# Inverse with needed columns only and its first products between the turns; four output tiles ended one by one, their next weights split first

## The chip, the cores and the metric

One Trainium2 chip; the program runs on 1 core. The metric is the device time of one execution in microseconds (us), lower is better.

## What is computed

Two small transformer stacks one after the other on 256 tokens (272 with 16 meta tokens), width 1024, all in float32: forgetting attention and a convolved FFN, a gated DeltaNet layer and another FFN, then an MLA layer and a MoBA layer.

```python
def first_block(x, meta_tokens, ...):
    h = jnp.concatenate([meta, x], axis=1)
    for i in range(DEPTH):                      # DEPTH = 2
        a = rmsnorm(h, norm_mix_pre[i])
        m = forgetting_attention(a, ...) if i % 2 == 0 else gated_deltanet(a, ...)
        h = h + rmsnorm(m, norm_mix_post[i])
        f = conv_ffn(rmsnorm(h, norm_ffn_pre[i]), ffn_w_up[i], ffn_conv[i], ffn_w_down[i])
        h = h + rmsnorm(f, norm_ffn_post[i])
    return h[:, N_META:]

def second_block(x, ...):
    for layer in range(DEPTH):
        y = mla_mixer(x, ...) if layer < N_A else moba_mixer(x, ...)   # each ends in ... @ w_o
        x = layer_norm(ALPHA * x + y, ln_g[layer], ln_b[layer])
    return x
```

The change touches two things in it: the products with the output weights of the four mixers (`@ w_out`, `@ w_o`), and, in the gated DeltaNet, the inverse of a unit triangular matrix that each chunk of each head needs.

## The kernel before

**Weights.** All weights stream through four buffers of 1024 columns (`raw`). For products in three passes each buffer is split: ScalarE copies it to `w_hi` in the rounded format (L359, `split_hi`), VectorE subtracts (`w_lo`, L364, `split_lo`), and TensorE makes hi*hi, hi*lo and lo*hi products (L378 to L380, `product`). A buffer may be split again only when its products are done (semaphore `chunk_used`); SyncE loads the next one when the lower half is done (`lo_done`).

**Output products.** An output weight has two units of four buffers; buffer `j % 4` makes output tile `j` of 8, over 8 blocks `k` of the input (24 products). Tiles 0 to 3 stand in four banks of PSUM. Tile 4 needs buffer 0 again, so it waits until tile 0 is done, then for the split. In `tail_pe` (attention, MLA, MoBA) tiles 0 to 2 are made up to `k = 6` between the steps of the last heads, then tile 3 up to `k = 6`, and then `k = 7` of all four. In the DeltaNet (`w_dn_out`) `k` is the outer loop, tiles 0 to 3 the inner one. In `out_act` (attention and DeltaNet) ScalarE copies a tile out (`m`, L677), squares it for the norm (`sq`, L680) and then splits the buffer; in `ln_act` (MLA, MoBA) it only splits, and VectorE copies out (L715).

**The inverse.** For each of 8 heads (`DNH`) there are 3 chunks of 96 rows. `d_in` holds the inverse so far, `d_tr` its transpose, `a_tr` the matrix. Blocks of 8 on the diagonal come first: `compact` gathers them (L1497), ScalarE copies them (`low`, L1784), seven products (L1519) feed a chain of 14 short VectorE instructions on `q_raw`/`k_raw`, and L1955 expands the result to `d_in`, one instruction a head. Then four levels double the block (8, 16, 32, 64). In a level, step `n` is one head: `x_of(n)` multiplies `a_tr` and `d_in` into `x` (L1534), VectorE masks it into `x_st` (L1967), `update(n)` multiplies `x_st` and `d_tr` (L1548), VectorE subtracts it from `d_tr` (L1979), and `turn(n)` transposes (L1557) so that ScalarE can renew `d_in` (L1791). All three stand in one loop of TensorE, shifted by two and three steps. Before level 1 all eight `turn`s of the expanded blocks run, since `x_of` waits for `d_in`'s semaphore. Levels 3 and 4 work on parts of the array (`part_of`: L1531, L1545, with VectorE's L1965 and L1977). Now and then a transpose of the values (`turn_values`, L1472) stands between.

`keep_clock(30, 3)` puts 30 products that nobody reads (L500) between the seven products and the turns. After the inverse the recurrence runs over the chunks (`c = 0, 1, 2`): three products a head for `c = 0` (L1602, L1610, L1614), five for `c = 1` (with L1588, L1609), four for `c = 2`; then the output product of the layer.

Of the kernel before, what the change touches and what calls it, by code (L numbers as in the profile page):

```python
# [9 lines left out]
ALU = mybir.AluOpType  # L10
# [35 lines left out]
def tables():  # L46
# [30 lines left out]
    def causal(blocks):  # L77
        parts = []
        for q0, q1 in blocks:
# [10 lines left out]
           for b in (BASE << n for n in range(LEVELS - 3))]  # L90
# [86 lines left out]
def build(nc, x, table, params, w, out):  # L177
# [7 lines left out]
    with ctx:  # L185
# [380 lines left out]
        def tail_pe(pe, f, wname, norm, cols, mean):  # L566
# [22 lines left out]
            part(3, 0, last)  # L589
            for j in range(4):  # L590
                part(j, last, KT)
            add(0)
# [75 lines left out]
        def out_act(act, wname, norm, cols):  # L668
# [3 lines left out]
            def tile(j, r):  # L672
                dst = bank[4 + r if "down" in wname else j % 4]
                if KIND[wname] == "down":
                    split(j)
                act.wait_ge(chunk_used, out_tile_done(wname, j))
# [4 lines left out]
                if KIND[wname] != "down":  # L681
                    split(j)
# [716 lines left out]
        def dn_pe(pe):  # L1399
# [112 lines left out]

# [8 lines left out]
            keep_clock(30, 3)  # L1521

            def x_of(n):
                pe.wait_ge(dn["d_in"], n - DNH + 1)
                wait(pe, dn["x_out"], n - DNH - 1)
                part = part_of(n)
                for c in range(NC):
                    cc = slice(c * C, (c + 1) * C)
                    if part:
                        lo, hi = part  # L1530
                        mm = nc.tensor.matmul(sub(bank[n % 2][hi], c, lo), sub(a_tr[lo, n % DNH, :], c, hi),  # L1531
                                              sub(d_in[lo, n % DNH, :], c, lo), start=True, stop=True)
                    else:
                        mm = nc.tensor.matmul(bank[n % 2][0:C, cc], a_tr[:, n % DNH, cc], d_in[:, n % DNH, cc], start=True, stop=True)  # L1534
                mm.then_inc(dn["x"], 1)

            def update(n):
                pe.wait_ge(dn["x_out"], n - DNH + 1)
                pe.wait_ge(dn["d"], n - 1)
                part = part_of(n)  # L1540
                for c in range(NC):
                    cc = slice(c * C, (c + 1) * C)
                    if part:
                        lo, hi = part
                        mm = nc.tensor.matmul(sub(bank[2 + n % 2][lo], c, hi), sub(x_slot(n)[hi], c, lo),  # L1545
                                              sub(d_tr[hi, n % DNH, :], c, hi), start=True, stop=True)
                    else:
                        mm = nc.tensor.matmul(bank[2 + n % 2][0:C, cc], x_slot(n)[:, cc], d_tr[:, n % DNH, cc], start=True, stop=True)  # L1548
# [10 lines left out]
            for n in range(LEVELS * DNH + 4):  # L1559
                if DNH <= n < LEVELS * DNH:  # L1560
                    x_of(n)
                if DNH <= n - 2 < LEVELS * DNH:
                    update(n - 2)
                back = n - (0 if n < DNH else 3)
                if n < DNH or DNH <= back < (LEVELS - 1) * DNH:
                    turn(back)
# [69 lines left out]
            for k in range(KT):  # L1636
                pe.wait_ge(dn["olo"], k + 1)
                for j in range(4):
                    out_part(pe, "w_dn_out", "post2", o_op, TAIL, None, False, j, [k])

# [183 lines left out]
        def dn_dve(dve, st):  # L1824
# [126 lines left out]
            for n in range(DNH):  # L1951
# [3 lines left out]
                nc.vector.tensor_tensor(full, own, blocks_of, ALU.mult).then_inc(dn["d"], 1)  # L1955
            for n in range(DNH, LEVELS * DNH + 2):
                if n < LEVELS * DNH:
                    lv = n // DNH
                    dve.wait_ge(dn["clear"], min(lv, LEVELS - 3))
                    wait(dve, dn["dd"], n - DNH - 1)  # L1960
                    dve.wait_ge(dn["x"], n - DNH + 1)
                    masks = tb("levels")[:, (lv - 1) * C:lv * C].unsqueeze(1).to_broadcast([C, NC, C]) if lv < LEVELS - 2 else None
                    if part_of(n):
                        lo, hi = part_of(n)
                        nc.vector.tensor_copy(sub_all(x_slot(n)[hi], lo), sub_all(bank[n % 2][hi, 0:TP], lo)).then_inc(dn["x_out"], 1)  # L1965
                    else:
                        nc.vector.tensor_tensor(lower(by_chunk(x_slot(n)), lv), lower(by_chunk(bank[n % 2][0:C, 0:TP]), lv),  # L1967
# [446 lines left out]
```

## Time and profile before

| | us |
|---|---|
| Median of 3 runs | 1238.79 (1238.43 to 1240.93) |
| The profiled execution, its own time | 1245.05 |
| Its span, first to last instruction | 1243.3 |
| TensorE busy in it | 1183.2 (95%) |
| VectorE busy | 854.2 (69%) |
| ScalarE busy | 707.2 (57%) |

Times in the trace are us from the start of the span. A row of the timeline is one instruction or several alike in a row: start, duration, engine and line, output and inputs, count; the brackets name how long the engine stood idle before it and who ended that. The profiler shows a float32 product as two records of TensorE (a transpose as one), so that three chunks give `x6`. "PEclk" is the granted TensorE clock: 1.00 is 2.4 GHz, 0.50 is 1.2 GHz.

### The profile page before, as it was taken

To read this page: it belongs to the slowest core of one execution; us is meant where nothing else is said; L and a number is where in the kernel's file an instruction comes from. 1 tells how busy PE (TensorE), PEld (TensorE's weight loads), DVE (VectorE), ACT (ScalarE), POOL (GpSimd) and SP (SyncE) were. 2 spreads that over 40 slices of the span, in tenths; PEclk is the share of its full clock that TensorE was granted. 3 is DMA by queue.
4 is the path that set the end of the run, shared out by engine and by line. 5 is a ranking of instruction groups with operands and counts; after the bars stand their busy time and mean duration, and the time that the engine had idled before them with its cause. 6 is when DMAs were issued, how large, how long until landed. Compare 5 with 4: busy or idle time off the path is not lost.

```text
span 1243.3 us, 27522 instructions
## 1 busy us (share of the span) xinstructions
PE 1183.2 (95%) x10101; PEld 1112.5 (89%) x10101; DVE 854.2 (69%) x1673; ACT 707.2 (57%) x1465; POOL 58.2 (5%) x64
## 2 busy tenths in 40 slices
PE   5999998999999999998998899999999999999996
PEld 4888887999999889988897799999988998899995
DVE  4888875777764487876434677875457876778874
ACT  6776755566654468664334566665545665555543
POOL 0000000122100000001000011110000000000000
PEclk9999998999999999998969899999999999999998
DMA  7333324355555444530100446556635443444431
GB/s 249 128 118 119 101 85 136 97 173 169 173 167 165 118 148 155 173 120 2 35 1 2 136 136 186 184 162 187 194 98 154 123 135 119 136 153 135 135 119 35
DMA packets 50087, 160.35 MB, mean 129 GB/s; under 512 B 5504, under 2 KB 8448, under 8 KB 49888
## 3 DMA queue, kind: packets, MB, share of 16 engines
q1 hardware_dynamic: 50016, 159.37, 41.3%
q8 instruction: 48, 0.79, 0.3%
q14 instruction: 23, 0.19, 0.0%
HBM read 158.30 MB, written 1.05 MB: 128 GB/s over the span
## 4 chain that ended last, share of the span: by engine, by line
PE 88%; DVE 5%; ACT 4%; issue 1%; DMA 1%; SPq 0%; POOL 0%; ACTq 0%; DVEq 0%
PE banks L378 24%; PE banks L380 22%; PE banks L379 22%; PE banks L500 2%; PE banks L917 2%; ACT w_hi L359 2%; PE banks L453 1%; PE banks L897 1%; DVE w_lo L364 1%; PE banks L882 1%; DVE m L533 1%; PE banks L1557 1%; PE banks L879 1%; PE banks L1602 1%; PE banks L1485 1%
## 5 line engine op out<-in xcount | busy, mean ns | idle before, releaser
L364 DVE TENSOR_TENSOR w_lo<-raw,w_hi 128x1024 fp32r<-128x1024 f32 (+5 forms) x332 | 370.2, 1121 | 194.1 <-ACT w_hi L359 193.0
L378 PE MATMUL banks<-x_hi,w_hi 128*128 128x272 f32 (+2 forms) x1624 | 477.7, 294 | 7.1 <-DVE x_lo L513 3.4
L379 PE MATMUL banks<-x_lo,w_hi 128*128 128x272 f32 (+2 forms) x1624 | 464.6, 286 | 0.0
L380 PE MATMUL banks<-x_hi,w_lo 128*128 128x272 f32 (+2 forms) x1624 | 464.4, 286 | 0.0
L359 ACT ACTIVATE w_hi<-raw 128x1024 fp32r<-128x1024 f32 (+5 forms) x332 | 314.5, 955 | 93.0 <-PE banks L380 87.1
L378 PEld LDWEIGHTS banks<-x_hi,w_hi 128*128 128x128 f32 x1624 | 307.4, 189 | 19.1 <-issue 9.1
L379 PEld LDWEIGHTS banks<-x_lo,w_hi 128*128 128x128 f32 x1624 | 308.4, 190 | 0.1
L380 PEld LDWEIGHTS banks<-x_hi,w_lo 128*128 128x128 f32 x1624 | 307.7, 189 | 0.0
L378 PE MATMUL banks<-hid_hi,w_hi 128*128 128x272 f32 (+1 forms) x352 | 101.3, 288 | 0.0
L380 PE MATMUL banks<-hid_hi,w_lo 128*128 128x272 f32 (+1 forms) x352 | 99.8, 284 | 0.0
L379 PE MATMUL banks<-hid_lo,w_hi 128*128 128x272 f32 (+1 forms) x352 | 99.8, 284 | 0.0
L1022 ACT ACTIVATE p_e<-s_m,mx 128x128 f32<-128x128 f32 (+3 forms) x112 | 48.0, 429 | 70.2 <-DVE mx L1126 70.2
L378 PE MATMUL banks<-o_hi,w_hi 128*128 128x256 f32 (+2 forms) x256 | 77.3, 302 | 6.7 <-DVE w_lo L364 5.5
L1381 POOL TENSOR_TENSOR hid<-g_e,u_y 128x272 f32<-128x272 f32 (+1 forms) x44 | 48.8, 1110 | 574.9 <-ACT g_e L1325 574.9
L380 PE MATMUL banks<-o_hi,w_lo 128*128 128x256 f32 (+2 forms) x256 | 73.8, 288 | 0.0
L379 PE MATMUL banks<-o_lo,w_hi 128*128 128x256 f32 (+2 forms) x256 | 73.7, 288 | 0.0
L1350 DVE SCALAR_TENSOR_TENSOR g_y<-banks,par,g_y 128x271 f32<-128x271 f32 (+1 forms) x88 | 43.3, 492 | 44.2 <-ACT u_y L1318 38.5
L378 PEld LDWEIGHTS banks<-hid_hi,w_hi 128*128 128x128 f32 x352 | 66.1, 188 | 1.1
L379 PEld LDWEIGHTS banks<-hid_lo,w_hi 128*128 128x128 f32 x352 | 66.4, 189 | 0.0
L380 PEld LDWEIGHTS banks<-hid_hi,w_lo 128*128 128x128 f32 x352 | 66.1, 188 | 0.0
L378 PEld LDWEIGHTS banks<-o_hi,w_hi 128*128 128x128 f32 x256 | 49.7, 194 | 10.5 <-issue 4.4
L379 PEld LDWEIGHTS banks<-o_lo,w_hi 128*128 128x128 f32 x256 | 49.7, 194 | 0.2
(303 smaller groups left out, 1770.2 us busy)
## 6 DMA issues: line engine op xcount, KB each, us to landing
raw<-w_up SPq DMA_DIRECT2D x88, 512.0 KB, 4.1
raw<-w_attn SPq DMA_DIRECT2D x32, 512.0 KB, 4.1
raw<-w_dn SPq DMA_DIRECT2D x32, 512.0 KB, 4.1
raw<-w_moba SPq DMA_DIRECT2D x32, 512.0 KB, 3.9
raw<-w_down SPq DMA_DIRECT2D x32, 384.0 KB, 3.2
raw<-w_down SPq DMA_DIRECT2D x32, 320.0 KB, 3.2
raw<-w_mla SPq DMA_DIRECT2D x16, 384.0 KB, 3.4
raw<-w_attn_out SPq DMA_DIRECT2D x8, 512.0 KB, 3.9
```

The costliest lines, as they stand in the source:

```text
L359: nc.scalar.activation(w_hi[:, q, 0:wd], raw[:, q, 0:wd], ACT.Copy).then_inc(hi_done, 1)
L364: nc.vector.tensor_tensor(w_lo[:, q, 0:wd], raw[:, q, 0:wd], w_hi[:, q, 0:wd].bitcast(F32), ALU.subtract).then_inc(lo_done, 1)
L378: nc.tensor.matmul(dst, hi, src[0][:, k, c0:c1], start=first, stop=False)
L379: nc.tensor.matmul(dst, hi, src[1][:, k, c0:c1], start=False, stop=False)
L380: return nc.tensor.matmul(dst, lo, src[0][:, k, c0:c1], start=False, stop=last)
L453: mm = nc.tensor.matmul(bank[where][ROW * g:ROW * (g + 1), 0:n_t], ones[:, 0:ROW], sq[:, slot, at:at + n_t], start=first, stop=last)
L500: nc.tensor.matmul(bank[at][:, 0:2 * P], ones_r, fixed_r[:, 0:2 * P], start=True, stop=True)
L533: marks.append(st(nc.vector.scalar_tensor_tensor(grouped(m[:, j, c0:c1]), grouped(m[:, j, c0:c1]), gain[:, j:j + 1], spread_of(cols), ALU. ...
L917: mm = nc.tensor.matmul(bank[5][64 * hh:64 * hh + 64, d0:d1], v_s[r, b, 64 * hh:64 * hh + 64], probs, start=i == 0, stop=i == len(part) - 1)
L1022: ins = nc.scalar.activation(p_e[r, hh, s0:s1], s_m[r, hh, s0:s1], ACT.Exp, bias=mx[r, hh, b:b + 1], scale=SCALE[f], accum_out=rs[r, hh, b ...
L1350: ins = nc.vector.scalar_tensor_tensor(y[:, r, lo:T], bank[2 * r + half][:, lo - back:T - back], conv_w(f, j, half, 2 - back), y[:, r, lo: ...
L1381: nc.gpsimd.tensor_tensor(hid[:, r, o0:T], g_e[:, r, o0:T], u_y[:, r, o0:T], ALU.mult).then_inc(prod_ready, 1)
```

## The change

- `tail_pe`: tile 3 goes only to `k = 3`, then `k = 7` ends tiles 0, 1 and 2, then tile 3 makes `k = 4` to `7`. For `w_dn_out` the outer loop over `k` ends at 5, and then each tile makes `k = 6, 7` on its own.
- `out_act`: for tiles 0 to 3 the split stands ahead of copy and square.
- Inverse: `x_of` at level 1 waits for the expanded blocks (`d`), not for `d_in`; the turns of the blocks stand in pairs between the first four `x_of`. VectorE expands three heads first and the others between the first steps.
- Products of a level stream only the columns that the level needs (half of them at levels 1 and 2, 32 and 64 of 96 at 3 and 4). Levels 3 and 4 have no parts any more: they load the whole 96x96 as the stationary operand, are masked, and GpSimd clears `x_st` for them too. The table has two masks more.
- `keep_clock(30, 3)` becomes `keep_clock(16, 3)`, and `keep_clock(8)` stands before the last `compact`.

```diff
@@ tail_pe
-            part(3, 0, last)
-            for j in range(4):
+            part(3, 0, 4)
+            for j in range(3):
                 part(j, last, KT)
+            part(3, 4, KT)
             add(0)
@@ out_act, tile
+                refill_first = KIND[wname] != "down" and j < 4
+                if refill_first:
+                    split(j)
                 act.wait_ge(chunk_used, out_tile_done(wname, j))
...
-                if KIND[wname] != "down":
+                if KIND[wname] != "down" and not refill_first:
                     split(j)
@@ dn_pe
             pe.wait_ge(dn["kt_out"], NC * DNH)
-
+            pe.wait_ge(dn["qn"], DNH)
+            keep_clock(8)
             pe.wait_ge(dn["at"], DNH)
             pe.wait_ge(dn["qk"], DNH)
             compact(DNH - 1)
...
-            keep_clock(30, 3)
+            keep_clock(16, 3)
 
             def x_of(n):
-                pe.wait_ge(dn["d_in"], n - DNH + 1)
+                if n < 2 * DNH:
+                    pe.wait_ge(dn["d"], n - DNH + 1)
+                else:
+                    pe.wait_ge(dn["d_in"], n - DNH + 1)
                 wait(pe, dn["x_out"], n - DNH - 1)
...
-                        mm = nc.tensor.matmul(bank[n % 2][0:C, cc], a_tr[:, n % DNH, cc], d_in[:, n % DNH, cc], start=True, stop=True)
+                    mm = nc.tensor.matmul(left(bank[n % 2][0:C, cc], n // DNH), a_tr[:, n % DNH, cc],
+                                          left(d_in[:, n % DNH, cc], n // DNH), start=True, stop=True)
...
-                        mm = nc.tensor.matmul(bank[2 + n % 2][0:C, cc], x_slot(n)[:, cc], d_tr[:, n % DNH, cc], start=True, stop=True)
+                    mm = nc.tensor.matmul(right(bank[2 + n % 2][0:C, cc], n // DNH), x_slot(n)[:, cc],
+                                          right(d_tr[:, n % DNH, cc], n // DNH), start=True, stop=True)
...
-            for n in range(LEVELS * DNH + 4):
-                if DNH <= n < LEVELS * DNH:
+            for n in range(DNH, LEVELS * DNH + 4):
+                if n < DNH + DNH // 2:
+                    turn(2 * (n - DNH))
+                    turn(2 * (n - DNH) + 1)
+                if n < LEVELS * DNH:
                     x_of(n)
@@ w_dn_out
-            for k in range(KT):
+            for k in range(KT - 2):
                 pe.wait_ge(dn["olo"], k + 1)
                 for j in range(4):
                     out_part(pe, "w_dn_out", "post2", o_op, TAIL, None, False, j, [k])
+            pe.wait_ge(dn["olo"], KT)
+            for j in range(4):
+                out_part(pe, "w_dn_out", "post2", o_op, TAIL, None, False, j, [KT - 2, KT - 1])
@@ dn_dve, every level
+                    nc.vector.tensor_tensor(lower(by_chunk(x_slot(n)), lv), lower(by_chunk(bank[n % 2][0:C, 0:TP]), lv),
+                                            lower(masks, lv), ALU.mult).then_inc(dn["x_out"], 1)
+                for k in range(expanded(n), expanded(n + 1)):
+                    expand(k)
...
+        EXPAND_AT = (3, 4, 6, 8)
@@ dn_pool
-            for lv in range(1, LEVELS - 2):
+            for lv in range(1, LEVELS):
                 pool.wait_ge(dn["block"], DNH)
+                if lv >= 3:
+                    pool.wait_ge(dn["dd"], (lv - 2) * DNH)
                 half = lv % 2 * 2
                 nc.gpsimd.memset(x_st[:, half:half + 2, :], 0.0).then_inc(dn["clear"], 1)
```

Two places in the order of instructions. First ScalarE in the attention output, right after its last work for the heads (`m` is the copy of an output tile, `sq` its square, `w_hi` the split of the next buffer). Before:

```order
L677 ACTIVATE m<-banks 128x272 [waits chunk_used]
L680 ACTIVATE sq<-banks 128x272 [waits sq_used]
L359 ACTIVATE w_hi<-raw 128x1024 [waits chunk_used,chunk0_loaded]
L677 ACTIVATE m<-banks 128x272 [waits chunk_used]
L680 ACTIVATE sq<-banks 128x272 [waits sq_used]
L359 ACTIVATE w_hi<-raw 128x1024 [waits chunk_used,chunk1_loaded]
```

And of the change:

```order
L359 ACTIVATE w_hi<-raw 128x1024 [waits chunk_used,chunk0_loaded]
L681 ACTIVATE m<-banks 128x272 [waits chunk_used]
L684 ACTIVATE sq<-banks 128x272 [waits sq_used]
L359 ACTIVATE w_hi<-raw 128x1024 [waits chunk_used,chunk1_loaded]
L681 ACTIVATE m<-banks 128x272 [waits chunk_used]
L684 ACTIVATE sq<-banks 128x272 [waits sq_used]
```

The split moved from behind copy and square to before them.

Second TensorE where the inverse begins (`q_raw`,`sq`: the seven products; `fixed_r`: keep_clock; `tab`,`d_in`: a turn, three chunks). Before:

```order
L1519 MATMUL banks<-q_raw,sq 96x24
L500 MATMUL banks<-fixed_r 128x256 x30
L1557 MATMUL banks<-tab,d_in 96x96 [waits dn_d]
L1557 MATMUL banks<-tab,d_in 96x96 x2
L1557 MATMUL banks<-tab,d_in 96x96 [waits dn_d]
L1557 MATMUL banks<-tab,d_in 96x96 x2
L1557 MATMUL banks<-tab,d_in 96x96 [waits dn_d_in,dn_d]
```

And of the change:

```order
L500 MATMUL banks<-fixed_r 128x256 [waits dn_qn,dn_kt_out]
L500 MATMUL banks<-fixed_r 128x256 x7
L1501 MATMUL banks<-tab,x_st 96x8 [waits dn_pair,dn_qk,dn_at]
...
L500 MATMUL banks<-fixed_r 128x256 x16
L1557 MATMUL banks<-tab,d_in 96x96 [waits dn_d]
L1557 MATMUL banks<-tab,d_in 96x96 x2
L1557 MATMUL banks<-tab,d_in 96x96 [waits dn_d]
L1557 MATMUL banks<-tab,d_in 96x96 x2
L1536 MATMUL banks<-d_in,a_tr 96x6x8 [waits dn_d]
L1536 MATMUL banks<-d_in,a_tr 96x6x8 x2
```

The first `x_of` (now L1536, 48 columns as 6x8) stands behind two turns instead of eight, and eight extra products stand ahead of the last `compact` (now L1501).

## Rows read from the trace of the kernel before

**Rows 1.** The page: busy time of TensorE, and its granted clock in 40 slices

```profile
PE 1183.2 (95%) x10101; PEld 1112.5 (89%) x10101; DVE 854.2 (69%) x1673; ACT 707.2 (57%) x1465; POOL 58.2 (5%) x64
...
PEclk9999998999999999998969899999999999999998
```

**Rows 2.** The page: the chain that ended last, by engine

```profile
PE 88%; DVE 5%; ACT 4%; issue 1%; DMA 1%; SPq 0%; POOL 0%; ACTq 0%; DVEq 0%
```

**Rows 3.** Timeline of the attention output: start us, us, engine, line

```profile
184.48 0.44 DVE L1202 TENSOR_TENSOR o_lo<-o_tmp,o_hi 128x272 fp32r<-128x272 f32 x1
...
186.86 0.40 ACT L677 ACTIVATE m<-banks 128x272 f32<-128x272 f32 x1 [4.92 <-PE banks L380]
187.15 0.39 ACT L680 ACTIVATE sq<-banks 128x272 f32<-128x272 f32 x1
187.43 1.06 ACT L359 ACTIVATE w_hi<-raw 128x1024 fp32r<-128x1024 f32 x1
...
189.89 0.36 PE L378 MATMUL banks<-o_hi,w_hi 128*128 128x272 f32 x1 [1.69 <-DVE w_lo L364]
190.10 0.29 PE L379 MATMUL banks<-o_lo,w_hi 128*128 128x272 f32 x1
```

**Rows 4.** Timeline of TensorE, the same place in DeltaNet and MLA output

```profile
683.74 0.36 PE L378 MATMUL banks<-o_hi,w_hi 128*128 128x260 f32 x1 [1.71 <-DVE w_lo L364]
683.93 0.28 PE L379 MATMUL banks<-o_lo,w_hi 128*128 128x260 f32 x1
684.05 0.28 PE L380 MATMUL banks<-o_hi,w_lo 128*128 128x260 f32 x1
...
1057.65 0.36 PE L378 MATMUL banks<-o_hi,w_hi 128*128 128x256 f32 x1 [1.06 <-DVE w_lo L364]
```

**Rows 5.** Windows around the stall at 188: us, TensorE busy, granted clock

```profile
187.00:190.60 3.60, 1.91 (x21) 1.00 0.00 0
190.60:194.00 3.40, 3.40 (x18) 0.51 0.83 239
```

**Rows 6.** Timeline of all engines where the inverse begins

```profile
574.76 0.65 PE L1497 MATMUL banks<-tab,x_st 96*96 96x8 f32 x6 [1.10 <-POOL x_st L2069]
...
578.08 6.08 PE L500 MATMUL banks<-fixed_r 128*128 128x256 f32 x30
...
580.54 3.04 DVE L1955 TENSOR_TENSOR d_in<-k_raw,tab 96x288 f32<-96x288 f32 x8
...
584.00 0.66 PE L1557 MATMUL banks<-tab,d_in 96*96 96x96 f32 x6
584.45 0.70 ACT L1791 ACTIVATE d_tr<-banks 96x288 f32<-96x288 f32 x2 [6.62 <-PE banks L1557]
```

**Rows 7.** Timeline of TensorE at level 1, one step between the first and last

```profile
590.90 0.41 PE L1557 MATMUL banks<-tab,d_tr 96*96 96x96 f32 x3
...
591.48 0.67 PE L1534 MATMUL banks<-d_in,a_tr 96*96 96x96 f32 x6
...
592.75 0.67 PE L1534 MATMUL banks<-d_in,a_tr 96*96 96x96 f32 x6
```

**Rows 8.** Windows: level 3, level 4 (two), c = 0, c = 1 (two): busy, clock

```profile
608.90:616.80 7.90, 7.81 (x127) 1.00 0.01 2
616.80:624.20 7.40, 7.40 (x97) 1.00 0.01 2
624.20:628.10 3.90, 3.33 (x28) 0.50 0.01 2
628.10:638.80 10.70, 10.67 (x48) 0.50 0.00 0
638.80:648.10 9.30, 9.29 (x45) 0.50 0.01 2
648.10:652.40 4.30, 4.30 (x40) 1.00 0.00 0
```

**Rows 9.** Timeline of TensorE in c = 1, first product of a head

```profile
642.58 0.63 PE L1588 MATMUL banks<-s_t,kq_all 128*96 128x128 f32 x2
...
644.72 0.63 PE L1588 MATMUL banks<-s_t,kq_all 128*96 128x128 f32 x2
...
648.53 0.38 PE L1588 MATMUL banks<-s_t,kq_all 128*96 128x128 f32 x2
...
649.64 0.38 PE L1588 MATMUL banks<-s_t,kq_all 128*96 128x128 f32 x2
```

More of the change, by code:

```diff
@@ L89, in tables @@
     lev = [((j // (2 * b) == i // (2 * b)) & (i % (2 * b) < b) & (j % (2 * b) >= b)) * 1.0
-           for b in (BASE << n for n in range(LEVELS - 3))]
+           for b in (BASE << n for n in range(LEVELS - 1))]
     t["levels"] = np.concatenate(lev, 1)
@@ L1538, in update @@
                 pe.wait_ge(dn["x_out"], n - DNH + 1)
-                pe.wait_ge(dn["d"], n - 1)
-                part = part_of(n)
+                pe.wait_ge(dn["d_in"], min(n - DNH + 1, DNH))
+                if n >= DNH + 2:
+                    pe.wait_ge(dn["d"], n - 1)
                 for c in range(NC):
                     cc = slice(c * C, (c + 1) * C)
[L1543 to L1547, printed above, removed]
-                        mm = nc.tensor.matmul(bank[2 + n % 2][0:C, cc], x_slot(n)[:, cc], d_tr[:, n % DNH, cc], start=True, stop=True)
+                    mm = nc.tensor.matmul(right(bank[2 + n % 2][0:C, cc], n // DNH), x_slot(n)[:, cc],
+                                          right(d_tr[:, n % DNH, cc], n // DNH), start=True, stop=True)
                 mm.then_inc(dn["dd"], 1)
@@ L1563, in dn_pe @@
                     update(n - 2)
-                back = n - (0 if n < DNH else 3)
-                if n < DNH or DNH <= back < (LEVELS - 1) * DNH:
-                    turn(back)
+                if DNH <= n - 3 < (LEVELS - 1) * DNH:
+                    turn(n - 3)
                 if turn_at(n) is not None:
@@ L1950, in dn_dve, with expand @@
                 st.settle()
-            for n in range(DNH):
+            def expand(n):
                 full = d_in[:, n, :].rearrange("p (c b t) -> p c b t", c=NC, t=BASE)
@@ L1955, in dn_dve @@
                 nc.vector.tensor_tensor(full, own, blocks_of, ALU.mult).then_inc(dn["d"], 1)
+            for n in range(EXPAND_AT[0]):
+                expand(n)
             for n in range(DNH, LEVELS * DNH + 2):
@@ L1973, in dn_dve @@
                     dve.wait_ge(dn["dd"], k - DNH + 1)
[L1974 to L1980 removed]
+                    nc.vector.tensor_tensor(upper(by_chunk(d_tr[:, k % DNH, :]), lv), upper(by_chunk(d_tr[:, k % DNH, :]), lv),
+                                            upper(by_chunk(bank[2 + k % 2][0:C, 0:TP]), lv), ALU.subtract).then_inc(dn["d"], 1)
             for c in range(NC):
@@ L2042, in by_chunk, with expanded @@
             return ap.rearrange("p (c t) -> p c t", c=NC)
+        EXPAND_AT = (3, 4, 6, 8)
+        def expanded(n):
+            return EXPAND_AT[min(n - DNH, len(EXPAND_AT) - 1)]
         def x_slot(n):
```

36 lines of the change are left out of this document (8 added, 28 removed).

## The prediction, made before the changed kernel ran

> **What bounds the kernel now.** I read the page first: TensorE is busy for 95% of the span and its granted clock is near full in all but a few slices [rows 1], and the chain that ended last is 88% TensorE [rows 2]. So only three things can move the time: a stall of TensorE that goes, work on TensorE that goes or comes, and time that it spends at the lower clock. The change touches four output products and the inverse, so I read those in the timeline, with the windows beside it for the clock.
>
> In the attention output TensorE stands idle for 1.69 us until the split of buffer 0 is done [rows 3]. Ahead of it stand a copy and a square of ScalarE (186.86 to 187.43, where the split starts), then the split of 1.06, then VectorE's half. The DeltaNet output has the same stall with 1.71, and the MLA output, where no copy stands ahead of the split, one of 1.06 [rows 4]; the MoBA output is built like MLA's, and I take the same for it. Around the first stall TensorE is busy for 1.91 us of 3.60, and in the 3.40 us behind it its clock is 0.51 [rows 5].
>
> In the inverse the 30 products of `keep_clock` run from 578.08 to 584.16, while the first expanded block is there at 580.54 + 3.04/8 = 580.92 [rows 6]. Then the turns run in pairs with ScalarE, and level 1 follows. A step there takes 592.75 - 591.48 = 1.27 us [rows 7], back to back.
>
> The largest thing is the clock. Levels 3 and 4 run at 1.00 until 624.2; from there the clock is 0.50 to 648.1, over the end of level 4, all of `c = 0` and most of `c = 1`, with TensorE nearly always busy [rows 8]. A head of `c = 1` takes 2.14 us at 0.50 and 1.11 at 1.00 [rows 9].
>
> **The four outputs.** Tile 0 ends nine products earlier than before: three tiles' last `k` stood behind three more blocks of tile 3, three products each; in the DeltaNet six products of each tile instead of three stand behind it. Products follow each other every 0.12 us [rows 4], so that is 1.1 us. In attention and DeltaNet the split also passes copy and square, 0.57 us [rows 3]. That makes 1.65 of the 1.69 and 1.71, and all of the two 1.06: 1.65 + 1.65 + 1.06 + 1.06 = 5.4 us. What could take it back: the last block of the head must be there nine products earlier. `o_lo` is done at 184.48 + 0.44 = 184.92, and tile 0's last products start 0.36 us before its copy at 186.86, so at 186.5, now at 185.4: half a microsecond is left. The square comes later by the split's 1.06 and earlier by 1.1, so the sum over tile 0, which TensorE makes before tile 4, finds it as before. In the DeltaNet all eight `o_lo` must be there before `k = 6`; by then TensorE has 72 products behind it, 8.6 us at least, and VectorE needs less than a microsecond for each. The buffers are free earlier, so the loads start earlier, which hurts nobody. With the first stall gone, the reason that I see for the 3.40 us at half clock is gone too: 3.40 x 0.49 = 1.7 us more. Bounds: 0 (it falls anyhow) and 1.7.
>
> **The start of the inverse.** `keep_clock(8)` stands where TensorE is idle for 1.10 us before the last `compact`, waiting for GpSimd [rows 6]. A product of 256 columns takes 6.08/30 = 0.20 us at half clock, so about 0.10 at full: 0.8 for eight, of which I let 0.3 stick out (bounds 0 and 0.8). Then 16 products at 0.20 end near 578.08 + 0.3 + 3.2 = 581.6, when the first blocks are there, against 584.00: 2.4 us gained. From 584.00 to the end of the second `update` at 590.90 before took 6.9 us [rows 6, 7]. The same work is 60 records of TensorE (8 turns of 3, 4 `x_of` and 2 `update` of 6), and a step of 15 records takes 1.27 us, 0.085 each: 5.1 us. ScalarE's two copies in a step, 0.70 [rows 6], fit in its 1.02. Gain 1.8. VectorE's later expansions are hidden under TensorE, two of 0.38 a step at most.
>
> **Half the columns.** Six records with 8 columns take 0.65 us [rows 6], six with 96 take 0.67 [rows 7]. So at the full clock it is not the streamed columns that set the pace but what both have in common, the load of 96 stationary columns. I cost halved columns at nothing for levels 1 and 2. The Trainium skill ("TensorE: Matmul & The Clock Gate", "LDWEIGHTS") says the same, that a load's time goes with its columns and not with its rows; but its section on what happens when a matmul is issued says that throughput is purely the number of streamed columns. By that rule alone halving them would pay, which is a rival below.
>
> **Levels 3 and 4.** They lose their small loads and now cost what a step of level 1 costs. Level 3: 8 x 1.27, and two transposes of values at 0.33 (591.48 - 590.90 less three records [rows 7]), 10.8 us against 7.9 [rows 8]: 2.9 lost. Level 4 has no turns: 8 steps of 12 records, 8.2; three late turns, 0.75; one transpose of values, 0.33; about 0.9 for the last mask, update and subtraction: 10.1 us against 7.4 + 3.9 = 11.3, of which 3.9 were at half clock: 1.2 gained. GpSimd's two further clears start when the level before last has ended, a whole level ahead; the masked instructions of VectorE have the columns of the copies before.
>
> **The recurrence.** Why did the clock fall at 624.2? TensorE was busy for 7.40 us of 7.40 just before [rows 8]; what was different from levels 1 and 2, which kept 1.00, was that the products used 32 or 64 rows and columns of the array. The change gives levels 3 and 4 the full 96x96. I take it that the clock then stays. `c = 0` took 10.7 us at 0.50 [rows 8]; by the ratio 1.11/2.14 = 0.52 [rows 9] that is 5.6, and with three products a head I leave 1.0 for hand-offs to ScalarE: 4.1 gained (bounds 0 and 5.1). The 9.3 us of `c = 1` at 0.50 become 4.8: 4.5 gained.
>
> **Sum.** -5.4 - 1.7 - 2.4 - 1.8 + 2.9 - 1.2 - 4.1 - 4.5 = -18.2 us. The profiled execution took 1245.05 with a span of 1243.3, so 1226.9 there; the median of the plain runs is 6.3 lower, 1238.8, and gives 1220.6. I forecast **1221**. Its own range, with the bounds above, is 1213 to 1228.
>
> **Rivals.**
> 1. *The clock falls again, late.* Fewer columns are streamed now, 32 per product at level 3, and nothing in the trace shows that 96x96 with few columns is enough. The clock would fall near the end of level 4 as before. Then the 8.6 us of the recurrence are not gained and some 1.5 of level 4 are lost: 1231. The Trainium skill (same page, "What's actually happening") says that the clock goes by how busy the engine has recently been; TensorE is as busy after as before, so by that rule alone nothing would change at this place. The trace disagrees in part: it fell at full business. Chance 0.14.
> 2. *The clock falls in level 3* (the one on the other side). Each step there is bound by loads, which take twice as long at half clock. The rest of level 3, about 5.4 us, and level 4's 10.1 double, and the recurrence gains nothing: 1220.6 + 15.5 + 8.6 = 1245. It decides for slower when more than 18.2 - 8.6 = 9.6 us of the levels run at half clock, so when it falls before level 4 begins. Chance 0.14.
> 3. *The clock is low when level 1 begins.* If the eight products keep the clock at full, sixteen end early, TensorE waits for VectorE near 580, and the fall comes then. All levels double, some 43 us, with the 8.6: about 1270. Against it: 16 at half clock reach 581.6, and in the trace the clock was back after the `keep_clock`. Chance 0.11.
> 4. *The outputs' gain is taken back* by later squares and sums: 1226 to 1228. Chance 0.08.
> 5. *Streamed columns set the pace after all.* Levels 1 to 3 would lose half of 12 records in each of 24 steps, 24 x 12 x 0.042 = 12 us: 1209. The 8-column rows speak against it. Chance 0.03.
>
> **The numbers.** The forecast has 0.50. Faster by over 0.2% (below 1236.3; 0.2% is what a measurement can tell here) are it, 1, 4 and 5, less a little: 0.73. Slower are 3 and most of 2: 0.22. Within 0.2%: 0.05. The range must take in 1, 4 and the nearer half of 2: 1213 to 1247.
>
> **What would show it.** Right: no idle time of TensorE for `w_lo` over 0.2 us in the four outputs and clock 1.00 at 190 to 194; first turn near 581.6; level 3 near 10.8 us; clock 1.00 from the turns through `c = 1`, whose heads take 1.11. Wrong: a half clock anywhere between 583 and 640 of the new trace, whose place tells rival 1, 2 or 3; steps of level 1 under 1.1 us (rival 5); new waits of TensorE for `sq` in the outputs (rival 4).

## The result, and the profile after the change

The kernel became slower: 1267.28 us median of 4 runs (1267.02 to 1268.59), beside 1239.86 (1238.43 to 1243.67) of the kernel before on the same chip. The ratio is 1.022, with a 95% interval of 1.019 to 1.024. The forecast was 1221.

The page of the changed kernel: TensorE is busier than before, and its clock is down in three slices in the middle (6, 5 and 5 tenths) where it was 8, 9 and 6 [rows 1].

```profile
PE 1210.0 (96%) x10095; PEld 1142.2 (90%) x10095; DVE 852.6 (67%) x1673; ACT 707.9 (56%) x1465; POOL 59.4 (5%) x66
...
PEclk9999999999999899996558999999999999999998
```

Its windows by stage, from the first turn: levels 1 to 4, `c = 0`, `c = 1`. After the stretch stand the length, TensorE's busy time (records), the same of weight loads, VectorE, ScalarE and GpSimd, then the granted clock, DMA share and GB/s:

```profile
574.75:597.00 22.25, 20.25 (x129) 19.46 (x130) 5.86 (x20) 6.29 (x15) 0.00 (x0) 0.53 0.00 1
597.00:617.50 20.50, 20.50 (x132) 20.44 (x130) 6.74 (x20) 4.50 (x12) 0.58 (x1) 0.50 0.18 52
617.50:637.30 19.80, 19.80 (x127) 19.76 (x127) 3.17 (x15) 3.31 (x10) 0.58 (x1) 0.50 0.00 1
637.30:656.90 19.60, 19.26 (x122) 19.10 (x120) 4.87 (x20) 1.48 (x5) 0.00 (x0) 0.50 0.01 1
656.90:667.60 10.70, 10.67 (x48) 10.33 (x49) 2.04 (x7) 4.85 (x16) 0.00 (x0) 0.50 0.00 0
667.60:680.20 12.60, 12.59 (x82) 12.24 (x81) 5.23 (x16) 4.74 (x17) 0.00 (x0) 0.71 0.01 1
```

The first stages of the kernel before, which had no such rows yet (levels 1 and 2, from its first turn at 584.00 [rows 6]; the others are in [rows 8]):

```profile
584.00:596.90 12.90, 11.93 (x132) 11.15 (x131) 3.20 (x13) 5.88 (x15) 0.00 (x0) 1.00 0.01 1
596.90:608.90 12.00, 11.60 (x131) 11.10 (x129) 6.67 (x20) 4.42 (x12) 0.00 (x0) 1.00 0.31 89
```

At levels 2 and 3 TensorE works without a pause, for 20.50 of 20.50 and 19.80 of 19.80 us, at a clock of 0.50. In the trace's record of the clock one stretch at half clock runs from 575.9 for 99.0 us, to 674.9. The span grew from 1243.3 to 1265.6, by 22.3, and the stages add up to that:

| | before | after | difference |
|---|---|---|---|
| up to the last `compact` | 574.76 | 568.53 | -6.2 |
| last `compact` to first turn | 9.24 | 6.22 | -3.0 |
| first turn to level 2 | 12.90 | 22.25 | +9.4 |
| level 2 | 12.0 | 20.5 | +8.5 |
| level 3 | 7.9 | 19.8 | +11.9 |
| level 4 | 11.3 | 19.6 | +8.3 |
| `c = 0` | 10.7 | 10.7 | 0 |
| `c = 1` | 13.6 | 12.6 | -1.0 |
| all behind | 590.9 | 585.4 | -5.5 |

So the stages ahead of level 1 and behind level 4 gained 15.7 us in all (none of it in `c = 0`), and the levels lost 38.1. The spans differ by less than the medians (22.3 against 27.4), since the profiled execution of the kernel before was a long one, 1245.05 where its other runs had 1238.43 to 1240.93. So some 5 us of those 15.7 probably belong to that execution and not to the change.

The outputs did what was forecast. Who waited for `w_lo`, in the view of L364 with its waits, TensorE's row before and then after (us, times):

```profile
PE banks L378: 7.7, 6
```

```profile
PE banks L378: 2.4, 3
```

That is 5.3 us less: the stalls of all four outputs are gone but for 0.16. The timeline shows it in the DeltaNet, where [rows 4] had 1.71, and the windows of the attention output, which answer to [rows 5], are busy throughout at full clock:

```profile
708.50 0.36 PE L378 MATMUL banks<-o_hi,w_hi 128*128 128x260 f32 x1 [0.16 <-DVE w_lo L364]
```

```profile
186.00:189.60 3.60, 3.60 (x42) 3.35 (x41) 3.01 (x3) 3.47 (x9) 0.00 (x0) 1.00 0.83 229
189.60:193.00 3.40, 3.40 (x41) 3.15 (x40) 1.48 (x2) 2.01 (x6) 0.00 (x0) 1.00 0.86 295
```

The timeline of all engines where the inverse begins answers to [rows 6]:

```profile
570.98 2.15 PE L500 MATMUL banks<-fixed_r 128*128 128x256 f32 x16
...
574.24 1.19 DVE L1960 TENSOR_TENSOR d_in<-k_raw,tab 96x288 f32<-96x288 f32 x3
574.75 0.62 PEld L1557 LDWEIGHTS banks<-tab,d_in 96*96 96x96 f32 x6 [1.82 <-DVE d_in L1960]
574.75 0.82 PE L1557 MATMUL banks<-tab,d_in 96*96 96x96 f32 x6 [1.62 <-DVE d_in L1960]
...
578.57 0.30 DVE L1970 TENSOR_TENSOR x_st<-banks,tab 96x144 f32<-96x144 f32 x1 [1.76 <-PE banks L1536]
578.80 0.81 DVE L1960 TENSOR_TENSOR d_in<-k_raw,tab 96x288 f32<-96x288 f32 x2
579.30 0.87 PEld L1557 LDWEIGHTS banks<-tab,d_in 96*96 96x96 f32 x6 [0.99 <-DVE d_in L1960]
579.30 1.20 PE L1557 MATMUL banks<-tab,d_in 96*96 96x96 f32 x6 [0.83 <-DVE d_in L1960]
```

The clock was still full during `keep_clock` (sixteen in 2.15 us, 0.13 each, against 6.08/30 = 0.20 before), so it ended early, TensorE stood idle for 1.62 us, and the half clock began at 575.9. Behind it TensorE waits for VectorE again, here 0.83: the expansions (L1960) stand behind a mask (L1970) that itself waits for TensorE.

### The profile page after: what moved, and what is told of

Read it like the earlier page. It is cut to its first block, busy times and chain, and to the rows that moved or that the text cites. A ratio compares the mean times of both kernels' runs of the same rounds, so it can differ in the third digit from the quotient of the medians.

```text
span 1265.6 us, 27514 instructions
## 1 busy us (share of the span) xinstructions
PE 1210.0 (96%) x10095; PEld 1142.2 (90%) x10095; DVE 852.6 (67%) x1673; ACT 707.9 (56%) x1465; POOL 59.4 (5%) x66
## 4 chain that ended last, share of the span: by engine, by line
PE 88%; DVE 6%; ACT 4%; issue 1%; DMA 0%; SPq 0%; ACTq 0%; DVEq 0%
PE banks L378 23%; PE banks L380 21%; PE banks L379 21%; PE banks L1547 2%; PE banks L1536 2%; PE banks L921 2%; PE banks L453 1%; ACT w_hi L359 1%; PE banks L1557 1%; PE banks L901 1%; PE banks L886 1%; PE banks L500 1%; DVE m L533 1%; DVE w_lo L364 1%; PE banks L883 1%
## 5 line engine op out<-in xcount | busy, mean ns | idle before, releaser
L364 DVE TENSOR_TENSOR w_lo<-raw,w_hi 128x1024 fp32r<-128x1024 f32 (+5 forms) x332 | 370.1, 1121 | 185.6 <-ACT w_hi L359 184.7
L1970 DVE TENSOR_TENSOR x_st<-banks,tab 96x144 f32<-96x144 f32 (+2 forms) x32 | 9.7, 304 | 60.4 <-PE banks L1547 57.9
```

The lines of the kernel that those rows point to most:

```text
L364: nc.vector.tensor_tensor(w_lo[:, q, 0:wd], raw[:, q, 0:wd], w_hi[:, q, 0:wd].bitcast(F32), ALU.subtract).then_inc(lo_done, 1)
```

## The experiments

Theories. **A**, my rival 3 as I had put it: the gap of 1.62 us makes the clock fall, and once it is low it stays low. **B**: products of half the columns don't keep the clock at full and don't bring it back, however busy TensorE is; the gap only decides when it falls. **C**: the order of turns and products, with its waits for VectorE, does it.

Three edits recur. *All columns*:

```diff
             def left(ap, lv):
+            if lv in FULL_COLS:
+                return ap
...
+        FULL_COLS = (1, 2, 3, 4)
```

(the same two lines in `right`). *Turns first*: all turns ahead of the first product as in the kernel before, and all expansions first on VectorE:

```diff
+            for n in range(DNH):
+                turn(n)
...
-                if n < DNH + DNH // 2:
-                    turn(2 * (n - DNH))
-                    turn(2 * (n - DNH) + 1)
...
-        EXPAND_AT = (3, 4, 6, 8)
+        EXPAND_AT = (8, 8, 8, 8)
```

*Keep 32*: `keep_clock(16, 3)` becomes `keep_clock(32, 3)`. Medians stand below with their lowest and highest, ratios are to the kernel before on the same chip with the 95% interval.

**The gap filled.** The changed kernel with *keep 32*:

```diff
-            keep_clock(16, 3)
+            keep_clock(32, 3)
```

> The changed kernel with 32 instead of 16 products of keep_clock ahead of the turns, nothing else. Theory A (the clock fell because TensorE stood idle for 1.6 us before the first turn, and the levels cannot raise it again): at the full clock 32 products take 3.4 us and reach the first expanded block, the clock stays 1.00 through the levels, c = 0 and c = 1, and the time is 1222 us (1216 to 1230). Rival B (the half columns or the order of the first steps pull the clock down by themselves): the half clock comes a few us later, in level 1 or 2, and the time is 1250 to 1267.

Measured: 1268.64 (1267.3 to 1269.5), ratio 1.022 (1.020 to 1.024). Its windows, from before the first turn:

```profile
574.00:580.70 6.70, 5.30 (x54) 4.84 (x52) 3.94 (x13) 2.10 (x6) 0.00 (x0) 1.00 0.00 0
580.70:596.00 15.30, 14.48 (x92) 14.28 (x92) 3.31 (x12) 4.07 (x10) 0.00 (x0) 0.50 0.00 1
```

The first turn now comes without a gap and at full clock, and the clock falls 5 us later all the same. And `keep_clock` as it was, without the eight ahead:

```diff
-            pe.wait_ge(dn["qn"], DNH)
-            keep_clock(8)
...
-            keep_clock(16, 3)
+            keep_clock(30, 3)
```

> The changed kernel with the clock-keeping products of before: none ahead of the last compact, 30 ahead of the turns. Theory A: the clock falls near the seven products as before, the 30 bring it back while they run, the first turn comes some 2.5 us later than it could, and from there the clock is 1.00 as in the trace of before at this place: 1225 us (1218 to 1233). Rival B: it falls again within level 1 or 2, 1250 to 1270.

Measured: 1269.36 (1267.63 to 1270.9), ratio 1.022 (1.020 to 1.024); half clock from 586.2 for 92.2 us. Theory A falls with these two: without the gap ahead of the first turn the time is the same.

**The outputs alone**, in the kernel before (the edits of `tail_pe`, `out_act` and `w_dn_out` only):

```diff
@@ tail_pe
-            part(3, 0, last)
+            part(3, 0, 4)
...
@@ w_dn_out
-            for k in range(KT):
+            for k in range(KT - 2):
...
```

> The kernel before with the edits of the four output products alone (tail_pe, out_act, w_dn_out), the inverse untouched. Both theories: the four stalls of 1.7, 1.7, 1.1 and 1.1 us go, and the 3.4 us at half clock behind the first: 7 us less than before, 1232 to 1234; the clock in the inverse as before (0.50 from level 4 to the middle of c = 1).

Measured: 1232.76 (1228.65 to 1234.87), ratio 0.994 (0.992 to 0.995). That is 7.8 us (5.7 to 9.9), against 5.4 + 1.7 forecast. The windows of [rows 5] are full, and `w_lo` is waited for as in the changed kernel (2.3 us, 3 times):

```profile
187.00:190.60 3.60, 3.60 (x43) 3.36 (x42) 2.45 (x2) 3.46 (x9) 0.00 (x0) 1.00 0.91 303
190.60:194.00 3.40, 3.40 (x41) 3.16 (x40) 1.25 (x2) 1.94 (x4) 0.00 (x0) 1.00 0.83 277
```

**`keep_clock` of 8 and 16 alone**, in the kernel before:

```diff
+            pe.wait_ge(dn["qn"], DNH)
+            keep_clock(8)
...
-            keep_clock(30, 3)
+            keep_clock(16, 3)
```

> The kernel before with nothing but the new counts of clock-keeping products: 8 ahead of the last compact, 16 instead of 30 ahead of the turns. Theory A: TensorE again stands idle before the turns, all levels of the old inverse run at half clock, and the time is 1255 to 1270. Rival B (the columns do it): the old levels with all columns keep or regain the clock, and the time is 1236 to 1240.

Measured: 1239.89 (1236.99 to 1245.08, 10 runs), ratio 0.9995 (0.998 to 1.001): no change that is clear of the noise, though the interval leaves room for a gain of 2.6 us. With all columns the levels 1 to 3 ran at full clock here, and the fall in level 4 stayed, 6.9 us into it where it was 7.4 in [rows 8], for 20.5 us:

```profile
602.60:610.50 7.90, 7.81 (x127) 6.28 (x126) 3.88 (x16) 3.36 (x11) 0.00 (x0) 1.00 0.01 2
617.40:632.80 15.40, 14.80 (x83) 13.82 (x81) 4.17 (x15) 4.85 (x16) 0.00 (x0) 0.50 0.00 1
```

From the last `compact` to the first turn its trace has 577.57 - 571.33 = 6.2 us, as the changed kernel has, and the kernel before has 9.2. But the trace of the outputs alone, where all 30 products still stand, has 573.88 - 567.60 = 6.3 too:

```profile
567.60 0.65 PE L1501 MATMUL banks<-tab,x_st 96*96 96x8 f32 x6 [1.17 <-POOL x_st L2076]
...
570.10 3.84 PE L500 MATMUL banks<-fixed_r 128*128 128x256 f32 x30
573.88 0.82 PE L1561 MATMUL banks<-tab,d_in 96*96 96x96 f32 x6
```

There the clock was full ahead of the turns (30 products in 3.84 us, not 6.08). So the 3.0 us of the table come from the clock of the profiled executions; fewer products gain them only in an execution whose clock is low there (with 16 the stretch was then 6.2 and 7.3 us, with 30 or 32 it was 9.2 to 9.5). Nor do the eight products decide that: in the traces of the kernels that have them the clock was full from the last `compact` to the first turn in nine and fell for a while in six.

**All columns in the changed kernel**, nothing else. Here B and C part:

```diff
+        FULL_COLS = (1, 2, 3, 4)
```

> The changed kernel, but every product of the four levels streams all 96 columns (the results outside the needed ones are not used); order, masks, clock-keeping products as changed. Theory B1 (half as many streamed columns is what lets the clock fall, and the stationary loads do not count): the clock is 1.00 in all levels, and the time is 1222 us (1216 to 1232). Theory B2 (the new order does it: in the first four steps TensorE waits 0.6 to 0.8 us three times for VectorE's expansions): the clock falls near the first steps all the same; with full columns it may come back, 1232 to 1267.

Measured: 1230.44 (1229.8 to 1233.05), ratio 0.991 (0.988 to 0.993). Its windows: the half-clock stretch, the rest of levels 1 and 2, level 3, level 4, `c = 0`, `c = 1`:

```profile
576.40:590.10 13.70, 11.70 (x71) 10.88 (x70) 3.47 (x11) 3.34 (x9) 0.00 (x0) 0.50 0.00 1
590.10:606.30 16.20, 15.79 (x181) 15.47 (x180) 8.16 (x26) 6.65 (x17) 0.58 (x1) 1.00 0.21 66
606.30:617.10 10.80, 10.80 (x129) 10.80 (x128) 3.19 (x16) 3.46 (x11) 0.57 (x1) 1.00 0.01 2
617.10:628.30 11.20, 10.61 (x122) 10.31 (x121) 4.97 (x20) 1.48 (x5) 0.00 (x0) 1.00 0.01 2
628.30:634.60 6.30, 6.07 (x49) 5.70 (x50) 2.04 (x7) 3.95 (x16) 0.00 (x0) 1.00 0.01 3
634.60:644.20 9.60, 9.36 (x82) 8.93 (x81) 4.89 (x16) 4.85 (x17) 0.00 (x0) 1.00 0.00 0
```

The gap and the waits are all still there and the clock falls in the same place, but it is back after 13.7 us instead of 99.0, and 37 us return. The number of records is the same; only columns were added. So the order alone (theory C) doesn't keep the clock down. And the other way round, **turns first with half the columns**:

> The changed kernel with the needed columns only, but all eight expansions and turns ahead of the first product, as before. B1: the clock still falls in level 1, 1262 to 1272 us. B2: it stays at 1.00 at least through levels 1 and 2, 1222 to 1240.

Measured: 1266.43 (1263.22 to 1268.27), ratio 1.019 (1.016 to 1.022). The order is that of the kernel before, the waits for expansions between the first steps are gone, and the clock stays down for 92.2 us, with TensorE busy almost without a pause. So the new order isn't needed for the loss:

```profile
578.30:590.00 11.70, 11.70 (x77) 11.68 (x76) 2.67 (x10) 2.67 (x7) 0.00 (x0) 0.50 0.01 1
590.00:670.00 80.00, 79.62 (x475) 78.64 (x475) 19.23 (x69) 16.09 (x49) 1.15 (x2) 0.50 0.05 14
```

**All columns at levels 1 and 2 only**, the needed ones at 3 and 4:

```diff
+        FULL_COLS = (1, 2)
```

> The changed kernel with all 96 columns at levels 1 and 2, and the needed ones (32 and 64 of 96) at levels 3 and 4. B1: the clock is 1.00 through levels 1 and 2 and falls in level 3, where only 32 columns are streamed: half of level 3 and all of level 4 at half clock, 1240 to 1250 us. If 96x96 loads with 32 columns were enough, 1222. B2: as in the first of these runs.

Measured: 1248.25 (1241.2 to 1251.45, 10 runs), ratio 1.006 (1.003 to 1.008). In the profiled execution (1242.79, among the shortest of the ten) level 3, with 32 of 96 columns, ran at full clock; then the clock fell in level 4, as before but 1.2 us into it instead of 7.4, for 30.7 us. That is the course of my rival 1, which had 1231 for it, at a higher cost:

```profile
604.80:615.40 10.60, 10.60 (x128) 10.60 (x127) 3.23 (x16) 3.49 (x11) 0.57 (x1) 1.00 0.01 2
616.60:634.00 17.40, 17.06 (x109) 16.91 (x107) 4.62 (x18) 1.23 (x4) 0.00 (x0) 0.50 0.01 1
```

**Turns first and all columns** (16 products of `keep_clock` as in the change):

> Both: all columns, and all turns ahead of the first product; of the inverse's change only the 96x96 products of levels 3 and 4, the masks and clears and the clock-keeping counts are left. B1 and B2 alike: clock 1.00 from the turns through c = 1. B1: 1.5 to 2 us over the run with full columns in the new order, 1224 us. B2: it is the faster of the two by 5 us or more.

Measured: 1228.56 (1226.39 to 1229.33), ratio 0.988 (0.986 to 0.991); half clock for 10.2 us from 576.6 and none after it in the inverse. **All columns, new order, keep 32**:

> All 96 columns in every product of the levels, new order of turns and products, and 32 instead of 16 clock-keeping products ahead of the turns. With 16 the clock fell for 13.7 us at the first steps and came back by itself. Theory A2 (that fall came from the 1.6 us in which TensorE stood idle before the first turn): it is gone, and 4 to 6 us with it: 1225 us. Theory A3 (the waits for VectorE's expansions between the first steps are enough to pull it down): a fall of 7 to 14 us remains, 1229 to 1231.

Measured: 1230.67 (1229.25 to 1233.64), ratio 0.993 (0.991 to 0.994). In its trace the clock was low for 6.8 us ahead of the turns and is full from the first turn on, with every wait for an expansion still there (11.89 us busy of 14.11), so those waits don't pull it down by themselves:

```profile
571.00:578.00 7.00, 7.00 (x36) 7.00 (x37) 4.78 (x17) 1.85 (x3) 0.58 (x2) 0.52 0.01 2
...
579.28:593.39 14.11, 11.89 (x132) 11.13 (x130) 5.01 (x17) 6.14 (x15) 0.00 (x0) 1.00 0.00 1
```

And **half the columns, turns first, keep 32**, the case without the gap ahead of the first turn and without the waits for expansions:

> The needed columns only, but no idle time of TensorE ahead of level 1: 32 clock-keeping products and all turns before the first product. B1 in its strong form (half the columns alone let the clock fall, with TensorE busy all the time): half clock within level 1, 1258 to 1270 us. If gaps of TensorE were needed for the fall, the clock stays 1.00 and the time is 1222 to 1230.

Measured: 1265.36 (1259.23 to 1270.52), ratio 1.021 (1.018 to 1.025). Its windows of level 1 (later part), the start of level 2, and the rest of level 2:

```profile
584.70:593.80 9.10, 9.05 (x109) 8.96 (x107) 3.18 (x13) 3.69 (x9) 0.00 (x0) 1.00 0.01 2
593.80:600.20 6.40, 6.16 (x74) 6.04 (x73) 3.62 (x11) 2.87 (x7) 0.57 (x1) 1.00 0.18 52
600.20:609.40 9.20, 9.20 (x61) 9.16 (x60) 3.19 (x9) 1.64 (x5) 0.00 (x0) 0.50 0.23 80
```

TensorE is busy for 9.05 of 9.10 and 6.16 of 6.40 us at full clock, and then the clock falls. So it isn't only that the clock isn't brought back with half the columns: it isn't held either, though it lasted from before the first turn through level 1. The stretch at half clock is 68.3 us long. The same kernel also shows what half the columns cost at full clock. In its timeline a step of level 1 goes from one turn to the next:

```profile
587.95 0.42 PE L1557 MATMUL banks<-tab,d_tr 96*96 96x96 f32 x3
588.20 0.49 PE L1476 MATMUL banks<-tab,v_all 128*96 128x128 f32 x3
588.53 0.63 PE L1536 MATMUL banks<-d_in,a_tr 96*96 96x48 f32 x6
...
589.51 0.42 PE L1557 MATMUL banks<-tab,d_tr 96*96 96x96 f32 x3
```

589.51 - 587.95 less the values' 0.33 is 1.23 us, against 1.27 with 96 columns [rows 7]. **All columns with turns first and keep 32** is the partner of that kernel:

> All 96 columns, all turns ahead of the first product, 32 clock-keeping products. Clock 1.00 from the turns to the end of c = 1. The 10.2 us at half clock of the same kernel with 16 products go: 1224 us. Against the new order with 32 products: 1.8 us slower by my count of TensorE's records, or faster if the waits for expansions in the new order cost more than they bring.

Measured: 1228.15 (1225.42 to 1229.96), ratio 0.990 (0.989 to 0.992), with no half clock in the whole inverse of its profiled execution.

**All columns in one of the two products** (`update`), the needed ones in `x_of`, keep 32:

```diff
             def right(ap, lv):
+            if lv in FULL_COLS:
+                return ap
```

> A dose between: x_of streams the needed columns (half at levels 1 and 2), update all 96; new order, 32 clock-keeping products. B1 with a fall that goes by the streamed columns: it lies between all (clock 1.00) and half (0.50 for 90 us). If three quarters are enough, 1225 to 1230 us; if not, 1250 to 1267.

Measured: 1268.68 (1268.48 to 1276.52), ratio 1.023 (1.022 to 1.025), half clock from 586.2 for 99.0 us in the profiled execution, which is the one of 1276.52. The kernel with all columns in both, and otherwise the same, took 1230.67: leaving out columns in one of the two is enough to lose the clock.

**The number of columns or their pattern?** The needed columns come in pieces (6x8 at level 1). Here all 96 are streamed, the needed pieces and then the others, at levels 1 and 2, and plainly at 3 and 4, with turns first:

```diff
             if lv <= 2:
+                return ap.rearrange("p (n a b) -> p a n b", a=2, b=b)
```

> The kernel with all turns first and 16 clock-keeping products (all 96 columns at levels 3 and 4), and at levels 1 and 2 all 96 columns too, but streamed in the order of the changed kernel: the needed ones first, as 6 pieces of 8 or 3 of 16, then the others. Theory N (the number of streamed columns decides over the clock): as the run with all columns in plain order, 1228 us (1225 to 1232). Theory S (the pieces, not the number, made the products weak): the half clock stays to the end of level 2 or longer, 1250 to 1267.

Measured: 1227.40 (1226.52 to 1229.61), ratio 0.989 (0.986 to 0.993); half clock for 6.8 us, then full. So at levels 1 and 2 it is their number, not their pattern.

**Columns put back that nobody reads**: half columns, turns first, and three products of 224 columns in each step:

```diff
             def x_of(n):
+                for _ in range(3):
+                    nc.tensor.matmul(bank[n % 2][:, TP:TP + 7 * 32], ones_r, fixed_r[:, 0:7 * 32], start=True, stop=True)
```

> The needed columns only, all turns first, 16 clock-keeping products, and in each of the 32 steps three products of 224 columns that nobody reads, ahead of x_of. If what TensorE streams decides, whatever it is for: the clock comes back in level 1 and stays, and the time is 1229 us plus some 0.3 us a step, 1232 to 1240. If the half products themselves hold the clock down: 1262 to 1285.

Measured: 7 of 11 executions took 1286.99 to 1291.85 us and 4 took 1240.06 to 1243.89, and the profiled one was of the first kind, so the kernel has two outcomes by the clock. In the profiled one:

```profile
576.30:695.80 119.50, 118.75 (x679) 116.73 (x677) 24.74 (x87) 22.39 (x64) 1.15 (x2) 0.50 0.03 10
```

Here the added columns didn't bring the clock back, although they are more (3 x 224 = 672 in a step) than the cut took out (twelve records of 48, 576); a step also became longer, 2.99 us (592.13 to 595.12), against 2.40 at half clock with all columns and no filler. The short executions have no trace; all that is known of them is the mean clock, 0.98 against 0.94, so they may have kept it through the inverse. This neither proves nor refutes B; it does say that adding up the columns of a step isn't enough to tell what the clock will do.

**Why the new order didn't gain.** From the first turn to level 2, at full clock and with all columns, the new order took 593.39 - 579.28 = 14.1 us and turns first 12.9. The timeline of the new order (the kernel with all columns and keep 32) names the waits:

```profile
581.28 0.45 PE L1557 MATMUL banks<-tab,d_in 96*96 96x96 f32 x3 [0.58 <-DVE d_in L1960]
...
583.08 0.82 PE L1557 MATMUL banks<-tab,d_in 96*96 96x96 f32 x6 [0.83 <-DVE d_in L1960]
...
585.73 0.82 PE L1557 MATMUL banks<-tab,d_in 96*96 96x96 f32 x6 [0.82 <-DVE d_in L1960]
```

They make 2.2 us. If they come from expansions that stand behind masks, then making all expansions first, under the same new order of TensorE, removes them (with keep 32 and all columns):

```diff
-        EXPAND_AT = (3, 4, 6, 8)
+        EXPAND_AT = (8, 8, 8, 8)
```

> The changed kernel with all 96 columns at every level and 32 columns of keep_clock, as before, and with the changed order of turns and products; VectorE makes all the expansions ahead of the masks and of I - T. If the changed order loses because TensorE waits for expansions that stand behind masks (0.58, 0.83 and 0.82 us in the kernel with the same columns and the same order), those waits go, the stretch from the first turn to level 2 falls from 14.1 us to some 12, and the time is near 1228. If TensorE then waits as long at the first step of level 1, for the masks, the stretch stays at 14 us and the time at 1230 or 1231.

Measured: 1224.00 (1223.56 to 1224.81), beside 1241.22 (1237.95 to 1246.21), ratio 0.986 (0.984 to 0.989), the lowest of all. VectorE's one row of expansions, and TensorE from the first turn to level 2:

```profile
575.10 3.04 DVE L1960 TENSOR_TENSOR d_in<-k_raw,tab 96x288 f32<-96x288 f32 x8
```

```profile
575.72:587.05 11.33, 11.33 (x131) 11.08 (x130) 5.42 (x19) 5.88 (x15) 0.00 (x0) 1.00 0.00 1
```

Not one idle moment in 11.33 us. That is 1.6 less than turns first, near the 1.8 that I had forecast for the change. Of the 6.7 us between this median and that of the same kernel with the expansions spread, 2.8 are this stretch; another 3.1 lie ahead of the first turn (6.4 us from the last `compact` against 9.4), where the other's trace had the clock low for 6.8 us, and aren't the edit's.

**The best order of the rest**: all columns, turns first, 8 and 24 products of `keep_clock`:

```diff
-            keep_clock(16, 3)
+            keep_clock(24, 3)
```

> All 96 columns at every level, all turns and all expansions first, keep_clock of 8 ahead of the expansion of the decays and of 24 behind it (8 and 16 left the inverse at half clock for 10 us, 32 at none). If 24 cover the gap, no half clock in the inverse and the earlier turns together give 1226 to 1228, with the four outputs' stall gone; if the clock falls at the 8, about 1229. Either is below both kernels.

Measured: 1228.85 median of 6 (five from 1225.74 to 1230.10, and one of 1623.13 that nothing here explains), ratio 0.990 (0.987 to 0.992). The first turn came at 577.0, with 3.4 us at half clock ahead of it; 12.9 us to level 2. No better than 32.

## Why the prediction was wrong

**The step that failed** stands under "The recurrence" and "Half the columns": "The change gives levels 3 and 4 the full 96x96. I take it that the clock then stays", and halved columns costed at nothing. I had looked at what the array holds. What the runs show in its place is that the clock hangs on the columns that the levels stream: with all 96 it holds at levels 3 and 4, in `c = 0` and `c = 1` (1.00 in the windows of the kernel with all columns); with the needed ones it falls even when it is full at the start, and isn't brought back, some 37 us. My rival 1 had named the few columns, but only for level 3; for levels 1 and 2 the question wasn't asked. The time of a step at full clock was right (1.23 to 1.27). That fits the statement of the Trainium skill ("TensorE: Matmul & The Clock Gate", "LDWEIGHTS") that I drew on, though no run here varied the stationary columns alone. By the rule of the same page ("What's actually happening"), that the clock goes by how busy the engine has been, it should have risen during 20.50 of 20.50 and 19.80 of 19.80 us of work. The trace disagrees.

**Rival 3** gave the right time (1270 for 1267) and the place to 4 us (near 580 for 575.9), and was held at 0.11. Its trigger was seen: sixteen products end early, TensorE waits. But it blamed the gap, and the gap is not the cause: without it the time is the same (1268.64), and with it, but with all columns, it is 1230.44. Its time had the clock stay low through all levels; the kernels with all columns brought it back in 7 to 14 us. So its number came out right in part by luck. My argument against it, that 16 at half clock reach 581.6, assumed half clock there; in the changed kernel's trace the clock was full, and as the experiments show, the eight products ahead don't settle which it is.

**Term by term:**

| term | forecast | shown |
|---|---|---|
| stalls in four outputs | -5.4 | waits for `w_lo` 7.7 to 2.4, -5.3 |
| clock behind the first | -1.7 | 1.00 there; both: -7.8 (-9.9 to -5.7) |
| earlier first turn | -2.4 | -3.0 in the trace, but so it is with 30 products at full clock; alone 0.9995 in time |
| products between turns | -1.8 | +1.2; -1.6 with expansions first |
| halved columns | 0 | -0.04 a step at full clock; the clock, some +37 |
| level 3, its length | 10.8 | 10.80 with all columns |
| level 4, its length | 10.1 | 11.20 with all columns |
| `c = 0` | -4.1 | 6.3 instead of 10.7, -4.4, with all columns |
| `c = 1` | -4.5 | 9.6 instead of 13.6, -4.0, with all columns |

Products between the turns: I wrote that VectorE's later expansions are hidden under TensorE. Their lengths would be; their place isn't, since VectorE takes its instructions in order and the masks ahead of them wait for TensorE. Level 4: I left out that the two last `update`s of level 3 still stand behind its first `x_of`, twelve records, 1.0 us. With the shown values the version with all columns and expansions first adds up to -5.3 - 1.7 - 2.9 - 1.6 + 2.9 - 0.1 - 4.4 - 4.0 = -17.1 (2.9 us is what its first turn came earlier, with 32 products at full clock), and it measured -17.2. That this is near the forecast's -18.2 is partly luck, since the first turn's share hangs on the clock of the execution.

**What stays open.** Why the clock goes by the columns that the levels stream isn't shown, and counts between these weren't tried, but for half in one product and all in the other. Nor is the number of columns of a product the whole of it: the last 18.0 us of the changed kernel's half clock (656.9 to 674.9) lie in `c = 0` and `c = 1`, whose products stream 96 and 128 columns, with TensorE busy for 10.67 of 10.70 and 7.29 of 7.30 us; in the kernel with all columns, where the clock came in full, the same products kept it. What decides whether the clock is low ahead of the turns isn't known either, nor why the kernel with three unread products a step has two outcomes.

## What to carry to other kernels

Work that is free at full clock isn't free to remove: before shortening a matmul whose time doesn't go by its columns, ask what keeps the clock up, and try the shortening alone. Read the granted clock beside the busy time, and don't take an unbroken row of small products for a reason that the clock is full. When a producer's work is cut into pieces and spread, look for what stands ahead of each piece on its engine and whom that waits for: two expansions of 0.81 us together behind a waiting mask cost TensorE 0.83. And before a shorter stretch of one trace is put down to an edit, look whether the clock in it was the same.

## What was unexpected

- With TensorE busy almost throughout, its clock stayed at 0.50 for 99.0 us, 81.0 of them in levels whose products stream 32 to 64 of 96 columns, and came back within 6.8 to 13.7 us with all 96, in the three kernels with all columns in whose trace it fell at the turns.
- At full clock a step with 48 columns takes 1.23 us and with 96 1.27. The Trainium skill ("TensorE: Matmul & The Clock Gate", "What happens when you issue a matmul") has throughput purely by the streamed columns; for these fp32 products of 96x96 the rows show next to none of that.
- The same kernel with unread products in each step took 1240 or 1288 us from one execution to the next.
- Ahead of the turns the clock was full or low for 3.4 to 6.8 us from trace to trace, in kernels whose instructions up to there are the same, and that moved the first turn by 3 us where 30 or 32 products of `keep_clock` stand.
